# A Trainium2 decoder-layer kernel: expert weights made per four rows, and the gathers, routing and key queries of the expert stage interleaved more finely

## The chip, the cores and the metric

The kernel runs on one core of one Trainium2 chip. The metric is the device time of one execution, in microseconds. The engines are named as in the profile: PE is TensorE, DVE is VectorE, ACT is ScalarE, POOL is GpSimd, SP is SyncE. Each engine works through its own instructions in order, and semaphores are what order one engine against another.

## The reference

One decoder layer on 256 tokens of width 1024: RMS norm, a combined projection, two groups of attention heads, an output projection and the residual, then a second RMS norm and a feed-forward part that looks up experts. Only that last part, PEER, is touched by the change:

```python
q = (xc @ w_query).reshape(PEER_CHUNK, PEER_HEADS, 2, PEER_D_HALF)
sc = jnp.einsum('chpd,hpnd->chpn', q, sub_keys)
s1, i1 = lax.top_k(sc[:, :, 0], 16)
s2, i2 = lax.top_k(sc[:, :, 1], 16)
cand = s1[..., :, None] + s2[..., None, :]
best, pos = lax.top_k(cand.reshape(..., 256), 16)
experts = take_along_axis(i1 * 128 + i2, pos)
g = softmax(best)
h = gelu(einsum('cd,chkd->chk', xc, u[experts]))
out = einsum('chk,chkd->cd', h * g, v[experts])
```

There are 8 heads, and each token takes 16 experts per head out of 16,384. An expert has one row of 1024 floats in u and one in v. So each of the 256 tokens reads 128 rows of u and 128 rows of v: 256 x 256 x 4 KB = 268 MB in all, the bulk of what the kernel moves.

## The kernel before

Tokens lie on the 128 partitions, in two halves h. Attention and both projections come first and are not touched. In the expert stage a **gather** is one indirect DMA from GpSimd: for a head i, a half h and a rank s it fetches one row of u (or of v) for each of 128 tokens, 128 x 4 KB = 512 KB. There are 8 x 2 x 16 = 256 U gathers and 256 V gathers, numbered n from 0 in the order head, half, rank. Head i's rows are 32 i to 32 i + 31. The work on them:

- TensorE makes the key queries (L1157, 16 projections of a head's half-query, `hp` = 0 to 15, two a head) and their products with the sub keys (`key_scores`, L1143), one after another for all heads. ScalarE copies both out of PSUM (`query_evac`, `scores_evac`). Only then do the V products start on TensorE, which takes its instructions in order. A projection chunk in `w_raw` serves two `hp`; SyncE loads the next one when `w_used` says that a slot is free.
- VectorE does `route(i)` for a head: top 16 of the keys of both halves (`top_keys`, twice), the top 16 of the sums (`top_candidates`), and the expert numbers (`experts`). `expert_ready` lets GpSimd gather the head's rows.
- GpSimd issues U gather n (L361) once `u_used` frees its slot in a ring of `U_RING` = 8 rows, and V gather n (L370) once `v_used` frees its slot in a ring of `V_RING` = 6 rows. Work goes in units of 16 rows (one head and half). In the loop over units it alternates one U gather of unit u with one V gather of unit u - 1, so that V runs 16 rows behind U. A wait of either kind holds all gathers behind it.
- VectorE takes the dot product of each U row with the normed token (`dots`, L904, a multiply with a sum, its two inputs both in SBUF), 16 in a row, then `weights(u)`: it waits for ScalarE's gelu of the 16 dots and multiplies by the softmax gate. After each even unit it does `route` of the next head in one piece.
- ScalarE turns each weight into a diagonal matrix (`diag`, L601, ring of 8), and TensorE adds diag times V row into four PSUM banks (L1175): two products of 128x512 per row, each recorded as two matmuls, so four records a row. The product's end raises `v_used`.

At the end the PSUM banks are copied to SBUF and stored.

Of the kernel before, what the change touches and what calls it, by code (L numbers as in the profile page):

```python
# [34 lines left out]
COLS = 512  # L35
TOPK = 16
PEER_HEADS = 8
N_KEYS = 128
HP = PEER_HEADS * 2
# [4 lines left out]
W_LOADS = 4  # L44
# [9 lines left out]
QK_TENSOR = [2, 3, 0, 1]  # L54
INSTANCES = MOBA_HEADS + 2 * DIFF_HEADS
MIXES = MOBA_HEADS + DIFF_HEADS
U_RING = 8
V_RING = 6
DIAG_RING = 8
PAIRS = HALVES * TOPK  # L60
GATHERS = PEER_HEADS * PAIRS
UNITS = PEER_HEADS * HALVES
G1, G2, GQK, GSUB = 0, 8, 16, 20
N_GAINS = 21

# [1 line left out]
def layer(nc, x, norm1_g, w_in, moba_g, diff_g, diff_lambda, subln_g, w_out, norm2_g, w_query, sub_keys,  # L67
# [59 lines left out]
    sk_nat = over.put("sk_nat", [P, HP, P])  # L127
    logits = over.put("logits", [P, 2, 3 * P])
    probsT = over.put("probsT", [P, 2, 3 * P])
    lam_in = over.put("lam_in", [P, 4 * HEAD])  # L130
    lam_prod = over.put("lam_prod", [P, 2, HEAD])
    tiny = {}
# [10 lines left out]
    expd = over.put("expd", [P, 4, 3 * P])  # L143
    mixed = over.put("mixed", [P, 2, 3 * P])
    w_lo = over.put("w_lo", [P, W_PARTS, 4, COLS], F32R)
    assert over.at <= arena_at

    over = Region(routing_at)
# [21 lines left out]
    with keep:  # L170
        ps = [keep.enter_context(nc.psum_tensor(f"bank{i}", [P, COLS], F32)) for i in range(8)]

        def sem(name):
            return keep.enter_context(nc.semaphore(name))
# [75 lines left out]
        diag_ready = sem("diag_ready")  # L250
        v_used = sem("v_used")
        y_ready = [sem(f"y_ready{h}") for h in range(HALVES)]

        def need(eng, s, value):

# [66 lines left out]
        def _(pool):  # L322
# [33 lines left out]
            def gather_u(n):  # L356

                i, pair = divmod(n, PAIRS)
                h, s = divmod(pair, TOPK)
                need(pool, u_used, n - U_RING + 1)  # L360
                pool.indirect_dma_start(u_rows[:, n % U_RING, :], None, peer_u[0],  # L361
                                        bass.IndirectOffsetOnAxis(ap=expert[:, i, h, s:s + 1], axis=0))\
                    .then_inc(u_landed[n % U_RING], 16)

            def gather_v(n):

                i, pair = divmod(n, PAIRS)
                h, s = divmod(pair, TOPK)
                need(pool, v_used, n - V_RING + 1)
                pool.indirect_dma_start(v_rows[:, n % V_RING, :], None, peer_v[0],  # L370
                                        bass.IndirectOffsetOnAxis(ap=expert[:, i, h, s:s + 1], axis=0))\
                    .then_inc(v_landed[n % V_RING], 16)

            for u in range(UNITS + 1):
                if u < UNITS and u % HALVES == 0:
                    pool.wait_ge(expert_ready, u // HALVES + 1)
                for s in range(TOPK):
                    if u < UNITS:
                        gather_u(u * TOPK + s)
                    if u:  # L380
                        gather_v((u - 1) * TOPK + s)

        @block.scalar
        def _(act):
# [181 lines left out]
            def scores_evac(hp):  # L566
                act.wait_ge(scores_done, hp + 1)
                act.activation(scores[:, :, hp, :], ps[hp % 2][:, 0:SEQ].rearrange("p (h n) -> p h n", h=2), ACT.Copy)\  # L568
                   .then_inc(scores_ready, 1)
# [7 lines left out]
            for hp in range(HP):  # L577
                query_evac(hp)
                if hp == 0:
                    scores_evac(0)  # L580
                elif hp > 1:
                    scores_evac(hp - 1)
            scores_evac(HP - 1)
# [6 lines left out]
            def gelu(u):  # L590

                i, h = divmod(u, HALVES)
                act.wait_ge(u_used, (u + 1) * TOPK)
                act.activation(h_gelu[:, i, h, :], h_dot[:, i, h, :], ACT.Gelu).then_inc(gelu_done, 1)  # L594

            def diagonal(n):

                i, pair = divmod(n, PAIRS)
                h, s = divmod(pair, TOPK)
                need(act, v_used, n - DIAG_RING + 1)  # L600
                act.activation(diag[:, n % DIAG_RING, :], ident[:, :], ACT.Copy, scale=act_w[:, i, h, s:s + 1])\  # L601
                   .then_inc(diag_ready, 1)

            gate_exp(0)
            for u in range(UNITS):
                gelu(u)
                act.wait_ge(act_ready, u + 1)
                for n in range(u * TOPK, (u + 1) * TOPK):
                    diagonal(n)
                if u % HALVES == 0 and u // HALVES + 1 < PEER_HEADS:  # L610
                    gate_exp(u // HALVES + 1)

            act.wait_ge(v_used, GATHERS - TOPK)
            for c in range(2):
# [5 lines left out]
        def _(dve):  # L620
# [267 lines left out]
            def route(i):  # L888

                top_keys(2 * i)  # L890
                values_at, last = top_keys(2 * i + 1)
                last = top_candidates(i, values_at)
                dve.wait_ge(dve_step, last)
                experts(i)
                dve.tensor_tensor(gexp[:, :, i, :], best[:, :, i, :], best[:, :, i, 0:1].to_broadcast([P, HALVES, TOPK]),
                                  ALU.subtract).then_inc(gexp_in, 1)

            def dots(u):

                i, h = divmod(u, HALVES)  # L900
                for s in range(TOPK):
                    n = u * TOPK + s
# [6 lines left out]
            def weights(u):  # L909

                i, h = divmod(u, HALVES)
                if h == 0:
# [5 lines left out]
                dve.wait_ge(gelu_done, u + 1)  # L918
                dve.tensor_tensor(act_w[:, i, h, :], h_gelu[:, i, h, :], gate[:, i % 2, h, :], ALU.mult).then_inc(act_ready, 1)

            dve.wait_ge(iota_ready, 1)
            route(0)
            dve.wait_ge(xg_ready, HALVES)
            for u in range(UNITS):
                dots(u)
                weights(u)
                if u % HALVES == 0 and u // HALVES + 1 < PEER_HEADS:
                    route(u // HALVES + 1)

            dve.wait_ge(v_used, GATHERS)  # L930
            dve.tensor_copy(y_rows[:, 1, 0:COLS], ps[6][:, :]).then_inc(y_ready[1], 1)
# [2 lines left out]
        def _(pe):  # L934
# [209 lines left out]
                             start=True, stop=True)  # L1144
                ins.then_inc(scores_done, 1)

            for hp in range(HP):
                c = hp % 2
                j = PROJ_CHUNKS + 4 + hp // 2
                if c == 0:  # L1150
                    pe.wait_ge(w_loaded[j % W_LOADS], 16 * (j // W_LOADS + 1))
                if hp >= 2:
                    pe.wait_ge(query_ready, hp - 1)
                for k in range(KD):
# [4 lines left out]
                ins.then_inc(query_done, 1)  # L1159
                if c == 1:  # L1160
                    pe.wait_ge(query_done, hp + 1)
                    pe.sem_inc(w_used, 1)
                if hp == 0:
                    key_scores(0)
                elif hp > 1:
                    key_scores(hp - 1)
            key_scores(HP - 1)

            for u in range(UNITS):
                h = u % HALVES  # L1170
                for n in range(u * TOPK, (u + 1) * TOPK):
                    pe.wait_ge(diag_ready, n + 1)
                    pe.wait_ge(v_landed[n % V_RING], 16 * (n // V_RING + 1))
                    for c in range(2):
                        ins = mm(ps[4 + 2 * h + c][:, :], diag[:, n % DIAG_RING, :],  # L1175
                                 v_rows[:, n % V_RING, c * COLS:(c + 1) * COLS],
                                 start=False, stop=True, skip_group_check=True)
                    ins.then_inc(v_used, 1)

# [22 lines left out]
```

## Time and profile before

| what | value |
|---|---|
| median of 3 runs | 911.74 us |
| lowest, highest | 909.52, 918.73 us |
| span of the profiled execution | 900.1 us, 6762 instructions |
| busy in the span | PE 701.9, DVE 499.7, ACT 222.0, POOL 564.0 us |
| software DMA queue (the gathers) | 268.47 MB |

The runs are whole executions. The profiled execution is one more, and of it the span is known, from its first to its last instruction; its device time is not listed beside it. The median lies 11.64 us above the span, which is taken as what lies around it. Busy time of an engine says what it did, not what the kernel waited for.

### The profile page before, as it was taken

Reading aid. Unit: us, or ns where it says so; the run is one execution under the profiler, and the core shown is the slowest. Engines: PE = TensorE matmul, PEld = TensorE weight load, DVE = VectorE, ACT = ScalarE, POOL = GpSimd, SP = SyncE. Lnnn points to the kernel's source line nnn. Section 1 sums busy time; section 2 is a strip of 40 time slices with the busy share of each in tenths; the row PEclk is TensorE's granted clock in tenths of the full one; section 3 lists DMA queues with packets and bytes.
Section 4 is the critical chain, followed back from the end, with each engine's and each line's share of the span. In section 5 each row is a group of like instructions: output and inputs, shape, how many; then the busy total and the mean of one; then the engine's idle time right before and its main releaser. Section 6 shows DMA issues by size and latency. Waiting matters only on the chain.

```text
span 900.1 us, 6762 instructions
## 1 busy us (share of the span) xinstructions
PE 701.9 (78%) x2005; PEld 338.8 (38%) x2005; DVE 499.7 (56%) x1224; ACT 222.0 (25%) x504; POOL 564.0 (63%) x535
## 2 busy tenths in 40 slices
PE   5999998997777667776767677777676777777788
PEld 4877787884222222222222222222222222222233
DVE  5577724654644754485449444944493559444420
ACT  6568742123110111021202120212021202111111
POOL 6001000573777777777777777777787777777762
PEclk9999999998799999999999999999999999999999
DMA  8744221795799999999999999999999999999996
GB/s 324 265 163 152 88 67 48 252 399 226 226 389 381 386 355 410 409 409 350 381 380 384 340 409 410 384 361 374 382 357 361 409 410 379 388 409 410 409 378 222
DMA packets 91974, 297.88 MB, mean 331 GB/s; under 512 B 8721, under 2 KB 17058, under 8 KB 91938
## 3 DMA queue, kind: packets, MB, share of 16 engines
q0 software_dynamic: 73728, 268.47, 77.7%
q1 hardware_dynamic: 18210, 28.98, 9.5%
q8 instruction: 17, 0.28, 0.1%
q14 instruction: 19, 0.16, 0.0%
HBM read 296.36 MB, written 1.05 MB: 330 GB/s over the span
## 4 chain that ended last, share of the span: by engine, by line
POOL 33%; PE 27%; DMA 20%; issue 12%; DVE 5%; ACT 2%; SPq 0%; DVEq 0%
DMA v_rows<-in_peer_v_dram,expert 19%; POOL u_rows L361 17%; POOL v_rows L370 16%; PE bank L1175 10%; PE bank L1157 6%; PE bank L957 5%; PE bank L1015 1%; PE bank L1143 1%; DVE w_lo L644 1%; DMA u_rows<-in_peer_u_dram,expert 1%; DVE t_nmax L674 1%; DVE logits L671 1%; DMA x_sb<-in_x_dram 0%; PE bank L942 0%; ACT diag L601 0%
## 5 line engine op out<-in xcount | busy, mean ns | idle before, releaser
L1175 PE MATMUL bank<-v_rows,diag 128*128 128x512 f32 x1024 | 506.9, 623 | 178.7 <-DMA v_rows<-in_peer_v_dram,expert 163.4
L904 DVE CUSTOM_DVE_ANT_0 u_rows<-u_rows,xg 128x1024 f32<-128x1024 f32 x256 | 310.4, 1226 | 283.7 <-DMA u_rows<-in_peer_u_dram,expert 283.4
L1175 PEld LDWEIGHTS bank<-v_rows,diag 128*128 128x128 f32 x1024 | 179.6, 193 | 505.4 <-issue 328.5
L361 POOL DMA_INDIRECT u_rows<-in_peer_u_dram,expert x256 | 269.3, 1052 | 105.1 <-issue 77.5
L370 POOL DMA_INDIRECT v_rows<-in_peer_v_dram,expert x256 | 274.7, 1073 | 94.9 <-issue 53.9
L601 ACT ACTIVATE diag<-ident,act_w 128x128 f32<-128x128 f32 x256 | 90.5, 394 | 273.3 <-PE bank L1175 267.4
L594 ACT ACTIVATE h_gelu<-h_dot 128x16 f32<-128x16 f32 x16 | 3.4, 216 | 282.0 <-DVE h_dot L904 282.0
L1157 PE MATMUL bank<-featT,w_raw 128*128 128x256 f32 x256 | 58.0, 380 | 0.7 <-ACT featT L563 0.4
L1157 PEld LDWEIGHTS bank<-featT,w_raw 128*128 128x128 f32 x256 | 47.4, 190 | 7.0 <-issue 1.3
L279 POOL TENSOR_TENSOR normed<-qk_raw,t_qk_rs 128x512 f32<-128x512 f32 x4 | 4.1, 1043 | 67.8 <-DVE t_qk_rs L740 67.8
L957 PE MATMUL bank<-w_hi,xn_hi 128*128 128x512 f32 x112 | 45.5, 406 | 0.2 <-DVE xn_lo L767 0.2
L957 PE MATMUL bank<-w_hi,xn_lo 128*128 128x512 f32 x112 | 43.8, 391 | 0.0
L957 PE MATMUL bank<-w_lo,xn_hi 128*128 128x512 f32 x112 | 43.7, 390 | 0.0
L644 DVE TENSOR_TENSOR w_lo<-w_raw,w_hi 128x2048 fp32r<-128x2048 f32 x16 | 36.6, 2289 | 9.8 <-ACT w_hi L396 9.8
L353 POOL IOTA iota<- 128x512 bf16 x1 | 0.6, 631 | 54.0 <-PE bank L1132 54.0
L396 ACT ACTIVATE w_hi<-w_raw 128x2048 fp32r<-128x2048 f32 x16 | 30.5, 1919 | 7.9 <-PE bank L957 4.1
L957 PEld LDWEIGHTS bank<-w_hi,xn_hi 128*128 128x128 f32 x112 | 21.0, 188 | 6.9 <-issue 3.1
L957 PEld LDWEIGHTS bank<-w_hi,xn_lo 128*128 128x128 f32 x112 | 21.0, 188 | 4.5
L957 PEld LDWEIGHTS bank<-w_lo,xn_hi 128*128 128x128 f32 x112 | 21.1, 188 | 4.1 <-issue 0.2
L904 DVE DVE_READ_ACCUMULATOR2_ANT h_dot<- 128x1 f32 x256 | 20.8, 81 | 0.0
L828 DVE MAX8 key_val<-scores 128x8 f32<-128x128 f32 x64 | 15.2, 280 | 7.6 <-ACT scores L568 7.6
L575 ACT ACTIVATE qT<-bank 128x256 f32<-128x256 f32 x16 | 6.1, 383 | 49.8 <-PE bank L1157 49.8
(149 smaller groups left out, 407.1 us busy)
## 6 DMA issues: line engine op xcount, KB each, us to landing
w_raw<-in_w_in_dram SPq DMA_DIRECT2D x12, 1024.0 KB, 8.4
w_raw<-in_peer_w_query_dram SPq DMA_DIRECT2D x8, 1024.0 KB, 5.4
w_raw<-in_w_out_dram SPq DMA_DIRECT2D x4, 1024.0 KB, 5.2
u_rows<-in_peer_u_dram,expert POOLq DMA_INDIRECT x256, 6.6
v_rows<-in_peer_v_dram,expert POOLq DMA_INDIRECT x256, 6.6
x_sb<-in_x_dram SPq DMA_DIRECT2D x2, 512.0 KB, 3.7
out_dram<-y_rows SPq DMA_DIRECT2D x2, 512.0 KB, 4.6
g_row<-in_norm_g_dram SPq DMA_DIRECT2D x1, 512.0 KB, 13.4
```

Of the source, the lines that this page charges most:

```text
L361: pool.indirect_dma_start(u_rows[:, n % U_RING, :], None, peer_u[0], bass.IndirectOffsetOnAxis(ap=expert[:, i, h, s:s + 1], axis=0))\
L370: pool.indirect_dma_start(v_rows[:, n % V_RING, :], None, peer_v[0], bass.IndirectOffsetOnAxis(ap=expert[:, i, h, s:s + 1], axis=0))\
L396: act.activation(w_hi[:, j % W_PARTS, :, :].rearrange("p k n -> p (k n)"), w_raw[:, j % W_LOADS, :], ACT.Copy)\
L601: act.activation(diag[:, n % DIAG_RING, :], ident[:, :], ACT.Copy, scale=act_w[:, i, h, s:s + 1])\
L644: dve.tensor_tensor(w_lo[:, j % W_PARTS, :, :].rearrange("p k n -> p (k n)"), w_raw[:, j % W_LOADS, :], w_hi[:, j % W_PARTS, :, :].rearran ...
L671: link(dve.tensor_tensor(logits[:, row, :], ps[bank][:, 0:3 * P], bias_t[:, table, :], ALU.add))
L674: ins = dve.tensor_reduce(tiny["nmax"][:, c:c + 1], logits[:, row, lo:hi], AX.X, ALU.max, negate=True)
L828: at[h] = mark(dve.max(val[h], scores[:, h, hp, :]))
L904: dve.tensor_tensor_reduce(out=u_rows[:, n % U_RING, :], in0=u_rows[:, n % U_RING, :], in1=xg[:, h, :], scale=1.0, scalar=0.0, op0=ALU.mul ...
L957: ins = mm(ps[bank][:, :], a[:, 4 * kh + k, h * P:(h + 1) * P], b[:, j % W_PARTS, k, :], start=start and k == 0 and n == 0, stop=stop and ...
L1157: ins = mm(ps[2 + hp % 2][:, 0:SEQ], w_raw[:, j % W_LOADS, 2 * k * P + c * P:2 * k * P + (c + 1) * P], featT[:, k, :], start=k == 0, stop= ...
L1175: ins = mm(ps[4 + 2 * h + c][:, :], diag[:, n % DIAG_RING, :], v_rows[:, n % V_RING, c * COLS:(c + 1) * COLS], start=False, stop=True, ski ...
```

## The change

- `U_RING` goes from 8 to 10 rows, `V_RING` from 6 to 8. To make room, three tiles of the attention part (`sk_nat`, `logits`, `probsT`) lie in the region that the rings use later.
- GpSimd alternates U gather n with V gather n - 8 (`LAG`) instead of n - 16.
- Weights are made in groups of four rows (`GROUP`): gelu on 4 dots, 64 times instead of 16. VectorE multiplies a group's weights after the dots of the next group.
- `route` is cut into four parts (the two `top_keys`, `top_candidates`, `experts` with the softmax input), placed after the dots of groups 1 to 4 of the eight groups of the head before.
- TensorE projects only `hp` 0 to 3 (heads 0 and 1) ahead of the V products. The projections and key scores of heads 2 to 7 stand between the V products of the head that is two earlier: half a projection after rows 1, 3, 5 and 7, key scores after rows 8 and 12. ScalarE's copies for them stand between its diagonals. The next chunk's load is released after row 12. Within heads 0 and 1 both projections now come ahead of both key scores.

```diff
-U_RING = 8
-V_RING = 6
+U_RING = 10
+V_RING = 8
+GROUP = 4
+LAG = 8
...
-            for u in range(UNITS + 1):
-                if u < UNITS and u % HALVES == 0:
-                    pool.wait_ge(expert_ready, u // HALVES + 1)
-                for s in range(TOPK):
-                    if u < UNITS:
-                        gather_u(u * TOPK + s)
-                    if u:
-                        gather_v((u - 1) * TOPK + s)
+            for n in range(GATHERS + LAG):
+                if n < GATHERS:
+                    if n % PAIRS == 0:
+                        pool.wait_ge(expert_ready, n // PAIRS + 1)
+                    gather_u(n)
+                if n >= LAG:
+                    gather_v(n - LAG)
...
+            for g in range(GROUPS + 1):
+                if g < GROUPS:
+                    gelu(g)
+                if g:
+                    act.wait_ge(act_ready, g)
+                    for n in range((g - 1) * GROUP, g * GROUP):
+                        diagonal(n)
+                        i, at = divmod(n, PAIRS)
+                        if i + 2 < PEER_HEADS:
+                            if at in (QUERY_EVAC, QUERY_EVAC + 4):
+                                query_evac(2 * (i + 2) + (at - QUERY_EVAC) // 4)
+                            if at in (SCORES_EVAC, SCORES_EVAC + 4):
+                                scores_evac(2 * (i + 2) + (at - SCORES_EVAC) // 4)
+                i, at = divmod(g, HEAD_GROUPS)
+                if at == 6 and i + 1 < PEER_HEADS:
+                    gate_exp(i + 1)
...
-            for u in range(UNITS):
-                dots(u)
-                weights(u)
-                if u % HALVES == 0 and u // HALVES + 1 < PEER_HEADS:
-                    route(u // HALVES + 1)
+            for g in range(GROUPS):
+                dots(g)
+                if g:
+                    weights(g - 1)
+                i, at = divmod(g, HEAD_GROUPS)
+                if 1 <= at <= 4 and i + 1 < PEER_HEADS:
+                    route(i + 1, at - 1)
+            weights(GROUPS - 1)
...
+            query(0, range(KD))
+            query(1, range(KD))
+            key_scores(0)
+            key_scores(1)
+            w_done(1)
+            query(2, range(KD))
+            query(3, range(KD))
+            key_scores(2)
+            key_scores(3)
+            w_done(3)
...
+                ins.then_inc(v_used, 1)
 
+                hp, at = 2 * (i + 2), n % PAIRS
+                if hp < HP:
+                    if at in (1, 5):
+                        query(hp + at // 4, range(4))
+                    if at in (3, 7):
+                        query(hp + at // 4, range(4, KD))
+                    if at in (8, 12):
+                        key_scores(hp + (at - 8) // 4)
+                    if at == 12:
+                        w_done(hp + 1)
```

## Rows read from the trace of the kernel before

**Rows 1.** The page's 40 slices of 22.5 us: GpSimd busy tenths, DMA rate.

```profile
POOL 6001000573777777777777777777787777777762
...
GB/s 324 265 163 152 88 67 48 252 399 226 226 389 381 386 355 410 409 409 350 381 380 384 340 409 410 384 361 374 382 357 361 409 410 379 388 409 410 409 378 222
```

**Rows 2.** The page's costliest groups: V products and dots.

```profile
L1175 PE MATMUL bank<-v_rows,diag 128*128 128x512 f32 x1024 | 506.9, 623 | 178.7 <-DMA v_rows<-in_peer_v_dram,expert 163.4
L904 DVE CUSTOM_DVE_ANT_0 u_rows<-u_rows,xg 128x1024 f32<-128x1024 f32 x256 | 310.4, 1226 | 283.7 <-DMA u_rows<-in_peer_u_dram,expert 283.4
```

**Rows 3.** Timeline of GpSimd (start us, us): first gathers, the stop.

```profile
165.76 1.16 POOL L361 DMA_INDIRECT u_rows<-in_peer_u_dram,expert  x1 [22.51 <-DVE expert L885]
...
178.08 1.19 POOL L361 DMA_INDIRECT u_rows<-in_peer_u_dram,expert  x1 [0.30 <-issue]
...
218.94 0.94 POOL L370 DMA_INDIRECT v_rows<-in_peer_v_dram,expert  x1 [10.98 <-PE bank L1175]
...
227.53 1.68 POOL L361 DMA_INDIRECT u_rows<-in_peer_u_dram,expert  x1 [5.09 <-DVE h_dot L904]
229.52 1.99 POOL L370 DMA_INDIRECT v_rows<-in_peer_v_dram,expert  x1 [0.30 <-issue]
```

**Rows 4.** Windows: busy us (count) by engine, granted clock, DMA share, GB/s.

```profile
350.00:370.00 20.00, 14.58 (x31) 4.82 (x29) 9.86 (x16) 3.21 (x8) 15.42 (x16) 1.00 1.03 409
433.00:468.00 35.00, 24.48 (x51) 8.32 (x49) 16.03 (x26) 5.06 (x15) 27.35 (x26) 1.00 1.00 377
488.00:498.00 10.00, 7.53 (x16) 2.41 (x14) 9.53 (x18) 1.61 (x4) 8.51 (x5) 1.00 0.89 316
```

**Rows 5.** Timeline, VectorE dots beside gathers: steady stretch, then one collision.

```profile
352.68 1.22 DVE L904 CUSTOM_DVE_ANT_0 u_rows<-u_rows,xg 128x1024 f32<-128x1024 f32 x1 [1.33 <-DMA u_rows<-in_peer_u_dram,expert]
...
353.70 1.01 POOL L361 DMA_INDIRECT u_rows<-in_peer_u_dram,expert  x1 [0.30 <-issue]
...
441.57 1.23 DVE L904 CUSTOM_DVE_ANT_0 u_rows<-u_rows,xg 128x1024 f32<-128x1024 f32 x1 [2.02 <-DMA u_rows<-in_peer_u_dram,expert]
...
441.90 1.70 POOL L370 DMA_INDIRECT v_rows<-in_peer_v_dram,expert  x1 [0.30 <-PE bank L1175]
```

**Rows 6.** Timeline, dots one behind another after routing, beside gathers.

```profile
402.84 1.22 DVE L904 CUSTOM_DVE_ANT_0 u_rows<-u_rows,xg 128x1024 f32<-128x1024 f32 x1
402.88 1.99 POOL L361 DMA_INDIRECT u_rows<-in_peer_u_dram,expert  x1 [0.30 <-issue]
...
403.98 1.22 DVE L904 CUSTOM_DVE_ANT_0 u_rows<-u_rows,xg 128x1024 f32<-128x1024 f32 x1
```

**Rows 7.** Windows of the U gathers alone, then of the V gathers alone.

```profile
229.52:858.80 629.28, 238.38 (x230) 0.98 1.00 383
...
229.52:858.80 629.28, 250.32 (x231) 0.98 1.00 383
```

**Rows 8.** Timeline, head 0's routing: second projection, its keys, candidates, experts.

```profile
147.62 3.62 PE L1157 MATMUL bank<-featT,w_raw 128*128 128x256 f32 x16
...
156.14 0.49 DVE L828 MAX8 key_val<-scores 128x8 f32<-128x128 f32 x2 [5.39 <-ACT scores L568]
...
158.49 0.17 DVE L840 TENSOR_TENSOR cand<-key_val 128x32 f32<-128x32 f32 x1
...
161.57 0.20 DVE L862 CAST key_idb<-key_idx 128x64 bf16<-128x64 uint32 x1
```

**Rows 9.** Timeline, the end: last U gather, last products, copy to SBUF.

```profile
858.82 1.01 POOL L361 DMA_INDIRECT u_rows<-in_peer_u_dram,expert  x1 [0.30 <-issue]
...
866.87 29.42 PE L1175 MATMUL bank<-v_rows,diag 128*128 128x512 f32 x68 [0.61 <-DMA v_rows<-in_peer_v_dram,expert]
...
896.33 0.60 ACT L617 ACTIVATE y_rows<-bank 128x512 f32<-128x512 f32 x1 [12.36 <-PE bank L1175]
```

**Rows 10.** Timeline of TensorE: a V product after an idle stretch.

```profile
234.88 3.75 PE L1175 MATMUL bank<-v_rows,diag 128*128 128x512 f32 x4 [3.35 <-DMA v_rows<-in_peer_v_dram,expert]
```

**Rows 11.** The view of one line, V gathers: time to landing.

```profile
DMA to landing us min/median/max: 4.3/6.6/8.1
```

More of the change, by code:

```diff
@@ L56 @@
 MIXES = MOBA_HEADS + DIFF_HEADS
-U_RING = 8
-V_RING = 6
+U_RING = 10
+V_RING = 8
 DIAG_RING = 8
+GROUP = 4
+LAG = 8
+QUERY_EVAC = 7
+SCORES_EVAC = 12
 PAIRS = HALVES * TOPK
 GATHERS = PEER_HEADS * PAIRS
-UNITS = PEER_HEADS * HALVES
+GROUPS = GATHERS // GROUP
+HEAD_GROUPS = PAIRS // GROUP
 G1, G2, GQK, GSUB = 0, 8, 16, 20
@@ L145, in layer @@
     w_lo = over.put("w_lo", [P, W_PARTS, 4, COLS], F32R)
+    sk_nat = over.put("sk_nat", [P, HP, P])
+    logits = over.put("logits", [P, 2, 3 * P])
+    probsT = over.put("probsT", [P, 2, 3 * P])
     assert over.at <= arena_at
@@ L252, in layer, with place @@
         y_ready = [sem(f"y_ready{h}") for h in range(HALVES)]
+        def place(n):
+            i, pair = divmod(n, PAIRS)
+            return i, *divmod(pair, TOPK)
         def need(eng, s, value):
@@ L575, in query_evac @@
                 act.activation(qT[:, hp % 2, :], ps[2 + hp % 2][:, 0:SEQ], ACT.Copy).then_inc(query_ready, 1)
-            for hp in range(HP):
+            for hp in range(4):
                 query_evac(hp)
-                if hp == 0:
+                if hp == 1:
                     scores_evac(0)
-                elif hp > 1:
-                    scores_evac(hp - 1)
-            scores_evac(HP - 1)
+                    scores_evac(1)
+            scores_evac(2)
+            scores_evac(3)
             def gate_exp(i):
@@ L588, in gate_exp, with gelu @@
                 act.activation(gexp[:, :, i, :], gexp[:, :, i, :], ACT.Exp).then_inc(gexp_done, 1)
[L590 to L594, printed above, removed]
+            def gelu(g):
+                i, h, s = place(g * GROUP)
+                act.wait_ge(u_used, (g + 1) * GROUP)
+                act.activation(h_gelu[:, i, h, s:s + GROUP], h_dot[:, i, h, s:s + GROUP], ACT.Gelu).then_inc(gelu_done, 1)
             def diagonal(n):
-                i, pair = divmod(n, PAIRS)
-                h, s = divmod(pair, TOPK)
+                i, h, s = place(n)
                 need(act, v_used, n - DIAG_RING + 1)
@@ L604, in _ @@
             gate_exp(0)
-            for u in range(UNITS):
[L606 to L609, printed above, removed]
-                if u % HALVES == 0 and u // HALVES + 1 < PEER_HEADS:
-                    gate_exp(u // HALVES + 1)
+            for g in range(GROUPS + 1):
[14 more added lines that the diff above has]
+                    gate_exp(i + 1)
             act.wait_ge(v_used, GATHERS - TOPK)
@@ L886, in experts, with route, dots @@
                                          ALU.mult, ALU.add).then_inc(expert_ready, 1)
[L888 to L902, printed above, removed]
+            values_at, positions_at = [0] * HP, [0] * PEER_HEADS
+            def route(i, part):
+                if part < 2:
+                    values_at[2 * i + part] = top_keys(2 * i + part)[0]
+                elif part == 2:
+                    positions_at[i] = top_candidates(i, values_at[2 * i + 1])
+                else:
+                    dve.wait_ge(dve_step, positions_at[i])
+                    experts(i)
+                    dve.tensor_tensor(gexp[:, :, i, :], best[:, :, i, :], best[:, :, i, 0:1].to_broadcast([P, HALVES, TOPK]),
+                                      ALU.subtract).then_inc(gexp_in, 1)
+            def dots(g):
+                for n in range(g * GROUP, (g + 1) * GROUP):
+                    i, h, s = place(n)
                     dve.wait_ge(u_landed[n % U_RING], 16 * (n // U_RING + 1))
@@ L907, in dots, with weights @@
                        .then_inc(u_used, 1)
-            def weights(u):
-                i, h = divmod(u, HALVES)
-                if h == 0:
+            def weights(g):
+                i, h, s = place(g * GROUP)
+                if g % HEAD_GROUPS == 0:
                     dve.wait_ge(gexp_done, i + 1)
@@ L917, in weights @@
                                            gsum[:, 1, i, :].unsqueeze(2).to_broadcast([P, HALVES, TOPK]), ALU.mult))
-                dve.wait_ge(gelu_done, u + 1)
-                dve.tensor_tensor(act_w[:, i, h, :], h_gelu[:, i, h, :], gate[:, i % 2, h, :], ALU.mult).then_inc(act_ready, 1)
+                dve.wait_ge(gelu_done, g + 1)
+                dve.tensor_tensor(act_w[:, i, h, s:s + GROUP], h_gelu[:, i, h, s:s + GROUP],
+                                  gate[:, i % 2, h, s:s + GROUP], ALU.mult).then_inc(act_ready, 1)
             dve.wait_ge(iota_ready, 1)
-            route(0)
+            for part in range(4):
+                route(0, part)
             dve.wait_ge(xg_ready, HALVES)
-            for u in range(UNITS):
-                dots(u)
-                weights(u)
-                if u % HALVES == 0 and u // HALVES + 1 < PEER_HEADS:
-                    route(u // HALVES + 1)
+            for g in range(GROUPS):
[6 more added lines that the diff above has]
+            weights(GROUPS - 1)
             dve.wait_ge(v_used, GATHERS)
@@ L1145, in key_scores, with query @@
                 ins.then_inc(scores_done, 1)
-            for hp in range(HP):
+            def query(hp, ks):
                 c = hp % 2
                 j = PROJ_CHUNKS + 4 + hp // 2
[L1150 to L1154, printed above, removed]
+                if ks[0] == 0:
+                    if c == 0:
+                        pe.wait_ge(w_loaded[j % W_LOADS], 16 * (j // W_LOADS + 1))
+                    if hp >= 2:
+                        pe.wait_ge(query_ready, hp - 1)
+                for k in ks:
                     if hp == 0 and k % 2 == 0:
@@ L1158, in _ @@
                              featT[:, k, :], start=k == 0, stop=k == KD - 1)
[L1159 to L1178, printed above, removed]
+                if ks[-1] == KD - 1:
+                    ins.then_inc(query_done, 1)
@@ new lines, in w_done @@
+            def w_done(hp):
+                pe.wait_ge(query_done, hp + 1)
+                pe.sem_inc(w_used, 1)
+            query(0, range(KD))
[8 more added lines that the diff above has]
+            w_done(3)
+            for n in range(GATHERS):
+                i, h, s = place(n)
+                pe.wait_ge(diag_ready, n + 1)
+                pe.wait_ge(v_landed[n % V_RING], 16 * (n // V_RING + 1))
+                for c in range(2):
+                    ins = mm(ps[4 + 2 * h + c][:, :], diag[:, n % DIAG_RING, :],
+                             v_rows[:, n % V_RING, c * COLS:(c + 1) * COLS],
+                             start=False, stop=True, skip_group_check=True)
+                ins.then_inc(v_used, 1)
[9 more added lines that the diff above has]
+                        w_done(hp + 1)
```

3 lines of the change are left out of this document (removed).

## The prediction

> **What bounds the kernel now.** I read the page's slices first [rows 1]. GpSimd's gathers start in the eighth slice (157 us); from the twelfth on it is busy seven or eight tenths and the DMA moves 340 to 410 GB/s. Between them, in slice 10, GpSimd falls to 3 tenths, and the rate to 226 GB/s for two slices. So four fifths of the span are the gathers. The groups [rows 2] say that the two engines that use the rows mostly wait for them: the dots' idle time, 283 us, ends with a U row's landing, and 163 of TensorE's 179 us with a V row's. The next question is whether GpSimd or the DMA sets the pace.
>
> The windows answer it [rows 4]. At 350 to 370 us the DMA moves 409 GB/s at a share of 1.03, so it is full: a row of 512 KB takes 1.28 us and a pair (one U, one V) 2.56. GpSimd's own floor is a hair under that: 0.94 us a gather and 0.30 to the next, 2.48 a pair [rows 3]. But the mean over 229.52 to 858.82 is 461 gathers in 629.3 us, 1.365 each: 1.06 us busy and 0.30 between [rows 7]. GpSimd never stops there; its gathers are longer than 0.94.
>
> The timeline says why. In the full stretch a U gather meets the last of a dot and takes 1.01. A gather that starts while a dot runs ends 0.80 us behind the dot: dot from 441.57 to 442.80, gather from 441.90 to 443.60 [rows 5]. With dots back to back each gather waits for one to end and the cycle is 1.99 + 0.30 = 2.29 [rows 6]. The Trainium skill (SBUF — State Buffer, "SBUF: two separate sides") has the shared port as an exclusive lock, the later one fully blocked. The trace agrees as to the gathers; if the dots too waited for whole gathers, a pair would be 1.22 + 2 x 0.94 + 0.60 = 3.7 us and not 2.56, so the lock holds only part of a gather.
>
> Two stretches are apart from this pace: the **stop** at 208 to 227, where GpSimd idles 10.98 us for the first V product (TensorE is still at queries) and then 5.09 us for the dots (VectorE is in `route`) [rows 3]; and the **end**, 858.82 to 896.3, where only V gathers are left and TensorE's 1.73 us a row (29.42 us for 17 rows) sets the rate [rows 9].
>
> **The change part by part**, along GpSimd's queue.
>
> Start. The second projection runs 147.62 to 151.24, yet its keys are read at 156.14, because its scores stand behind projection 2 [rows 8]. Now scores 0 and 1 follow projection 1. Without the gap ahead of it that ends at about 150.1; evacuations and scores bring the first `top_keys` to 151.5; one takes 158.49 - 156.14 = 2.35 us, the second starts at about 154.0, 2.1 us earlier. The first gather, 165.76 [rows 3], moves to **163.6**.
>
> U alone. 16 U gathers alone become 8. The first eight took 178.08 - 165.76 = **12.3 us** [rows 3], beside loads of query weights, of which two of four now come later.
>
> Stop. V gather 8 would be the first to wait for V product 0. It is due 16 gathers after 175.9, at 197 us. Product 0 wants dots 0 to 7, a group's weights and a diagonal: by about 185. TensorE is then free since about 161, so the wait and the stop go (16 us). TensorE starts cold: a product after idle took 3.75 us instead of 1.95 [rows 10]. With 12 us in hand and a ring of 8 a few such rows cost nothing.
>
> Pairs. From U gather 8 to U gather 255 there are 247 pairs, 494 gathers. At today's 1.365 they take 674 us. What moves that pace:
> - `route` in parts. It takes 2 x 2.35 + 3.08 (158.49 to 161.57) + about 4 = 11.8 us [rows 8], and holds the dots: eight back to back follow, four gathers of 1.05 us excess, 4.2 us a head. In parts nothing of it goes: 11.8 us of dots' delay still make about 7 displaced dots. At 0.52 us each (1.05 per two dots, rows 6) that is 3.6 us. Single delays of 1 us can hide in the DMA queue, whose landing time of 6.6 us lies 2.3 above its least [rows 11]. I take 1 us a head off, 7 us.
> - The pace between them has two modes in the trace, full DMA at 1.28 a gather and 377 GB/s, 1.39 a gather [rows 4], where dots hit every third V gather. Which one follows a disturbance I can't read; bounds 1.29 and 1.40.
> - 48 more gelus (ACT has idle time; it makes diagonals up to 8 ahead) and 48 more weight products of 0.18 us. These fall into the 1.33 us for which VectorE waits before each dot [rows 5]. Uncovered: 8 us of VectorE, nothing of GpSimd. As two-input operations they can hold a gather 0.18 us; bounds 0 and 8 us, taken 0, since few meet one.
> - Projections between products: a head costs TensorE 32 x 1.73 + 2 x 3.6 + 1.2 = 64 us of the 82 to 88 that its gathers take, at worst 2 to 3 us late against 11 us of slack in V's ring (8 x 2.7 less landing and product). ScalarE's diagonal behind a `query_evac` waits for TensorE's third row; eight diagonals are ahead. 0 us; without the cover the bound is still 64 a head, below the gathers.
> - Rings of 10 and 8: GpSimd shows no wait for a slot outside the stop, so 0. What they give is cover.
> - Two query chunks of 1 MB now load beside full gathers: 0 if there is slack, 5.1 us at 409 GB/s; taken 2.5.
>
> So the pairs take 494 x 1.35 = **667 us**, and the last U gather starts at 163.6 + 12.3 + 667 + 2.5 = 845.4.
>
> End. It leaves 9 V gathers at 1.28. The first lands at about +7.9 us; nine products of 1.73 follow: TensorE ends at +23.5. Copy and store take 900.1 - 896.3 = 3.8 [rows 9]. That is **27.3** where 41.3 stands now.
>
> Sum: 845.4 + 27.3 = 872.7 us of span; with 11.64 around it, **884 us**, against 911.74. The same by part: start -2.1; the first 33 gathers, 63.8 us up to 229.52 with the stop in them [rows 3], now 12.3 + 25 x 1.35 = 46.1, so -17.7; eight V gathers more ahead of the last U gather, +10.8; pace of the other 461, -7; loads +2.5; end -14. That is -27.4.
>
> **The rivals.**
> 1. **Full DMA takes over.** With short disturbances the mode of 1.28 holds. For it: 350 to 370, and VectorE no longer stays away 12 us. Against: half the dots of a head are displaced. At 1.295: 494 x 0.055 = 27 less, 857 us. Chance 0.20.
> 2. **More collisions.** Each part kicks the phase between dots and gathers, and 377 GB/s becomes the rule: 1.40, 25 more, 909 us. Chance 0.18.
> 3. **Slower: dots back to back become normal.** If 20 of 32 dots of a head cost 0.52 us (pair 3.0) and 12 stay at 2.73, the pair is 2.90: 1.45 x 494 puts 49 us on the sum, 933 us. Beyond 1.425 a gather it passes 921. Against: after 4 us of routing VectorE needs only two or three dots to catch up. Chance 0.07.
> 4. **The stop stays**, from a late first weight or cold TensorE: 16 us back, 900. Chance 0.05.
>
> The skill's table on the same page ("A bandwidth-pool intuition that's wrong") gives a core about 358 GB/s from HBM. By it 268 MB need 750 us and no finer order would help; the time would stay at or above today's. The row with 409 GB/s over 20 us stands against it, so this rival gets no chance of its own.
>
> **How the numbers follow.** The forecast 884 has 0.50. The range runs from 858, the full-DMA case, to 909, the colliding one; it leaves out the rest of rival 3 and part of the two edges. A change under 1% (9 us) is about what can't be told from none here. Faster by over 1% (below 902.6): 0.50 + 0.20 + 0.05 + 0.06 of rival 2 = 0.81. Within: 0.12 of rival 2 and 0.01 = 0.13. Slower: 0.06.
>
> **What would show it.** The first gather at about 163.6; GpSimd with no idle over 1 us after it; V gathers from about 176; gathers 1.29 to 1.40 us apart on the mean, 1.35 as forecast; four short runs of two or three back-to-back dots a head in place of one of eight, gathers of 1.99 fewer; last U gather near 845 with under 28 us behind it. Wrong would be: GpSimd waiting for a ring or for `expert_ready`, VectorE waiting for gelu behind a ScalarE that is held by a query, or a mean gather above 1.12 us busy.

## The result, and the profile after

| | before | changed |
|---|---|---|
| median | 911.46 us (4 runs) | 888.88 us (4 runs, 887.01 to 890.03) |
| ratio of the changed kernel to the one before | | 0.973, 95% interval 0.9674 to 0.9785 |
| span of the profiled execution | 900.1 us | 888.2 us |

The changed kernel is 22.6 us faster, 2.7%. The forecast was 884 with a range of 858 to 909. (Medians are over all executions; the ratios here and below leave out every execution that took over 1.5% longer than the fastest of its kernel.) The profiled execution of it took 890.03 us, 1.8 around its span. For the one before, its executions beside the later runs have spans too, and on the first two chips each lies 1.7 to 2.0 us under its time (906.41 with 904.5, for one). So its profiled execution, with a span of 900.1, was some 9 us shorter than its median, and the 11.64 us that the prediction put around the span were mostly that difference.

Where the time went is read best along GpSimd's queue. First the page's slices, as in [rows 1]:

```profile
POOL 6001000577777777777777777777777777777772
...
GB/s 329 268 149 150 88 71 65 237 365 367 404 410 371 356 404 409 377 346 365 376 368 370 400 388 372 352 409 408 389 369 372 373 377 369 382 372 370 402 409 255
```

The hole in the tenth and eleventh slices is gone. The level of the rest is not higher: it moves between 350 and 410 as before. The timeline of GpSimd gives the start, which answers to [rows 3]:

```profile
162.97 1.16 POOL L371 DMA_INDIRECT u_rows<-in_peer_u_dram,expert  x1 [19.73 <-DVE expert L902]
...
174.20 0.99 POOL L371 DMA_INDIRECT u_rows<-in_peer_u_dram,expert  x1 [0.30 <-issue]
175.50 1.39 POOL L380 DMA_INDIRECT v_rows<-in_peer_v_dram,expert  x1 [0.30 <-issue]
```

174.20 is U gather 8, behind the eight that go alone; 175.50 is V gather 0. From there to the end no gather has more than 0.31 us of idle ahead of it. The windows of the U gathers alone and of the V gathers alone, from the first V gather to the last U gather, answer to [rows 7]:

```profile
175.50:860.61 685.11, 251.31 (x247) 0.99 1.00 381
...
175.50:860.61 685.11, 283.48 (x247) 0.99 1.00 381
```

These windows hold 494 gathers, of which the last one only starts at their end. So from V gather 0 to U gather 255 there are 493 intervals in 685.11 us, and from U gather 8, where the prediction begins its pairs, 494 in 686.41: 1.39 us each, 1.085 of it busy. The profiled execution of the kernel before had 1.365. The end, as in [rows 9]:

```profile
860.61 1.02 POOL L371 DMA_INDIRECT u_rows<-in_peer_u_dram,expert  x1 [0.30 <-issue]
...
868.66 15.69 PE L1210 MATMUL bank<-v_rows,diag 128*128 128x512 f32 x36 [0.61 <-DMA v_rows<-in_peer_v_dram,expert]
...
884.38 0.60 ACT L634 ACTIVATE y_rows<-bank 128x512 f32<-128x512 f32 x1 [12.35 <-PE bank L1210]
```

Nine products (36 records) end the work, where there were 17. 27.6 us lie behind the last U gather, where there were 41.3.

The sum of the changed kernel, term by term, forecast against measured:

| stretch | forecast | measured |
|---|---|---|
| to the first gather | 163.6 | 162.97 |
| eight U gathers alone | 12.3 | 11.23 |
| 494 gathers in pairs | 667 | 686.41 |
| query loads beside them | 2.5 | in the line above |
| behind the last U gather | 27.3 | 27.6 |
| span | 872.7 | 888.2 |
| around the span | 11.64 | 1.8 |

Two errors, 15.5 us too little in the span and 9.8 too much around it, stand against each other in the 884.

The timeline of TensorE shows the cold start that rival 4 feared:

```profile
182.05 5.76 PE L1210 MATMUL bank<-v_rows,diag 128*128 128x512 f32 x8 [22.73 <-DMA v_rows<-in_peer_v_dram,expert]
187.65 1.89 PE L1184 MATMUL bank<-featT,w_raw 128*128 128x256 f32 x8
189.38 3.60 PE L1210 MATMUL bank<-v_rows,diag 128*128 128x512 f32 x8
```

After 22.73 us of idle the first two rows take 5.76 us, at a mean granted clock of 0.64 from 182 to 188 us, and the next two 3.60, at 1.00 from 188 us on; half a projection between them costs 1.7 us. V gather 8 found its slot free: it went out at 199.10, 0.30 us behind the gather ahead of it.

And the timeline of dots and gathers shows what holds the pace, after a part of the routing:

```profile
371.34 1.20 DVE L924 CUSTOM_DVE_ANT_0 u_rows<-u_rows,xg 128x1024 f32<-128x1024 f32 x1
371.35 2.00 POOL L380 DMA_INDIRECT v_rows<-in_peer_v_dram,expert  x1 [0.31 <-PE bank L1210]
```

The gather that starts with the dot takes 2.00 us instead of 0.94. The runs of seven to nine dots back to back are gone (there were seven of them), but V gathers are busy 1.148 us on the mean of this stretch (283.48 / 247), against 1.084 before (250.32 / 231 in [rows 7]), while U gathers go from 1.036 to 1.022 (251.31 / 246, without the one at the end). Fewer gathers are held for a whole dot (15 take over 1.9 us instead of 25), but more are held for a part of one: 86 take over 1.3 us instead of 62.

### The profile page after: what moved, and what is told of

It is laid out like the page before. It is cut to its first block, busy times and chain, and to the rows that moved or that the text cites. A ratio compares the mean times of both kernels' runs of the same rounds, so it can differ in the third digit from the quotient of the medians.

```text
span 888.2 us, 6905 instructions
## 1 busy us (share of the span) xinstructions
PE 687.9 (77%) x2005; PEld 340.3 (38%) x2005; DVE 504.3 (57%) x1272; ACT 215.6 (24%) x552; POOL 574.4 (65%) x535
## 4 chain that ended last, share of the span: by engine, by line
DMA 29%; POOL 29%; PE 24%; issue 11%; DVE 5%; ACT 1%; SPq 0%; POOLq 0%; DVEq 0%
DMA v_rows<-in_peer_v_dram,expert 29%; POOL u_rows L371 15%; POOL v_rows L380 14%; PE bank L1210 13%; PE bank L982 5%; PE bank L1184 2%; PE bank L1040 1%; DVE w_lo L661 1%; DVE t_nmax L691 1%; DVE logits L688 1%; DMA x_sb<-in_x_dram 0%; PE bank L967 0%; PE bank L1005 0%; DVE expd L716 0%; PE bank L1001 0%
## 5 line engine op out<-in xcount | busy, mean ns | idle before, releaser
L1210 PE MATMUL bank<-v_rows,diag 128*128 128x512 f32 x1024 | 499.0, 613 | 183.5 <-DMA v_rows<-in_peer_v_dram,expert 176.3
L380 POOL DMA_INDIRECT v_rows<-in_peer_v_dram,expert x256 | 292.1, 1141 | 78.1 <-issue 46.3
L371 POOL DMA_INDIRECT u_rows<-in_peer_u_dram,expert x256 | 262.1, 1024 | 97.5 <-issue 77.8
L603 ACT ACTIVATE h_gelu<-h_dot 128x4 f32<-128x4 f32 x64 | 13.1, 205 | 551.9 <-DVE h_dot L924 551.9
L609 ACT ACTIVATE diag<-ident,act_w 128x128 f32<-128x128 f32 x256 | 81.9, 387 | 4.1 <-DVE act_w L939 4.1
L848 DVE FIND_INDEX8 key_idx<-key_val,scores 128x8 uint32<-128x128 f32 x64 | 17.7, 283 | 0.0
```

The costliest lines, as they stand in the source:

```text
L603: act.activation(h_gelu[:, i, h, s:s + GROUP], h_dot[:, i, h, s:s + GROUP], ACT.Gelu).then_inc(gelu_done, 1)
L848: last = mark(dve.max_index(key_idx[:, h, hp, 8 * r:8 * r + 8], val[h], scores[:, h, hp, :]))
```

## The experiments

The theory was: the stop and the end gave the gain; the pace between is set by dots that hold gathers, and the change left that alone. Rivals were that the projections between products or the cut routing slow the pairs, and that the pace is the DMA's own. The first four kernels each undo one part of the changed kernel; they share one chip and its runs of the kernel before (median 911.2 us).

**All queries ahead of the V products again.**

```diff
-            query(0, range(KD))
-            query(1, range(KD))
-            key_scores(0)
-            key_scores(1)
-            w_done(1)
...
+            for i in range(PEER_HEADS):
+                query(2 * i, range(KD))
+                query(2 * i + 1, range(KD))
+                key_scores(2 * i)
+                key_scores(2 * i + 1)
+                w_done(2 * i + 1)
```

> Undoes the placing of the queries alone: TensorE makes all 16 projections ahead of the first V product. Theory (the stop is TensorE's queue, the pace between is set by dots that hold gathers): the stop comes back at V gather 8, near 197 us, until the first product near 208 us, so 10 to 16 us of idle GpSimd and a time 8 to 14 us above the changed kernel's 889, about 900. The pace of the pairs stays at 1.37 to 1.40 us a gather. Rival (projections between V products are what slows the pairs to 1.39): the pace falls to 1.35 or less and the time comes out at or below 889.

Measured: 904.67 us median, 0.9931 of the kernel before (0.9887 to 0.9976). Its timeline of GpSimd:

```profile
195.41 0.94 POOL L371 DMA_INDIRECT u_rows<-in_peer_u_dram,expert  x1 [0.30 <-issue]
215.04 1.03 POOL L380 DMA_INDIRECT v_rows<-in_peer_v_dram,expert  x1 [18.69 <-PE bank L1204]
```

The stop is back, in one piece of 18.69 us at V gather 8, and the time is 15.8 us above the changed kernel's; both are just above the expected 10 to 16 and 8 to 14. TensorE's first V product came at 211.12, after 4.23 us of waiting for its diagonal, and it was cold (granted clock 0.57 from 211 to 215 us): V gather 8 went out at 215.04, after it. Without the stop the 493 intervals of the pairs are 1.388 us each, as in the changed kernel (1.390). So the projections cost the pairs nothing that shows, and moving them is worth the stop.

**The routing in one piece again**, after the dots of group 3.

```diff
-                if 1 <= at <= 4 and i + 1 < PEER_HEADS:
-                    route(i + 1, at - 1)
+                if at == 3 and i + 1 < PEER_HEADS:
+                    for part in range(4):
+                        route(i + 1, part)
```

> Undoes the cutting of the routing alone: all four parts stand after the dots of group 3. Theory (a dot that is displaced costs the same, in one run or in four): pace 1.37 to 1.41 us a gather as in the changed kernel, time within 1% of 889. Rival (the four kicks of a head knock the dots out of the mode of 1.28 a gather): the pace falls to 1.365 or lower, 12 us or more off, 877 or less.

Measured: 880.23 us (878.24 to 885.16), 0.9675 (0.9622 to 0.9727), at a pace of 1.362. Here the theory missed: the time lies at the edge of the 1%, and the pace is better by 0.028 and below the 1.37 expected. It is the pace that the rival named, but not its time. The interval of the ratio overlaps that of the changed kernel (0.9674 to 0.9785). The page's groups of gathers:

```profile
L371 POOL DMA_INDIRECT u_rows<-in_peer_u_dram,expert x256 | 266.2, 1040 | 97.5 <-issue 77.7
L380 POOL DMA_INDIRECT v_rows<-in_peer_v_dram,expert x256 | 275.7, 1077 | 78.1 <-issue 48.2
```

V gathers take 1.077 us instead of the changed kernel's 1.141 over the whole execution, U gathers 1.040 instead of 1.024. 58 gathers take over 1.3 us, where the changed kernel has 86.

**V 16 rows behind U again.**

```diff
-LAG = 8
+LAG = 16
```

> Undoes the lag alone: V gathers 16 behind U gathers again. Theory (end and start are worth 14 and 18 us less 11 for the V gathers that move): 17 V gathers are left after the last U gather and go at TensorE's 1.73 us a row, so the part behind the last U gather grows from 27.6 to about 41, and the last U gather starts about 11 us less 2 to 3 for slower single U gathers earlier: 893 to 896 us, up 4 to 7. Rival (the lag is worth nothing, since the work is the same): within 2 us of 889.

Measured: 892.47 us, 0.9839 (0.9743 to 0.9934), within 1 us of the expectation; one of its four executions took 905.57. The last U gather starts at 848.97, 11.6 us before the changed kernel's, and 41.2 us follow it; 17 products stand in a row at the end of TensorE's timeline:

```profile
856.99 29.42 PE L1210 MATMUL bank<-v_rows,diag 128*128 128x512 f32 x68 [0.60 <-DMA v_rows<-in_peer_v_dram,expert]
```

The pace is 1.386. So the lag moves 14 us out of the end and puts 11 into the pairs, as the traces show. The net of 3.6 us between the medians is smaller than the noise: the intervals of the two ratios overlap.

**Rings of 8 and 6 rows again**, in the same memory.

```diff
-U_RING = 10
-V_RING = 8
+U_RING = 8
+V_RING = 6
```

> Undoes the ring sizes alone: 8 and 6 rows are used. Theory (GpSimd never waits for a slot): no idle of GpSimd over 1 us behind the first gather, time within 1% of 889. Rival (the larger rings are what covers the projections between products and the routing): idle on GpSimd before V or U gathers, over 9 us in sum, 898 or more.

Measured: 892.78 us (888.96 to 900.38), 0.9801 (0.972 to 0.9882), pace 1.394. Only the last three V gathers wait, 1.6 us at most, which is over the 1 us expected but lies in the end and not in the pairs. The rings are worth nothing here that can be told from chance.

The next three test what sets the pace; they share another chip (kernel before 911.9 us there).

**Half dots.**

```diff
-... tensor_tensor_reduce(out=u_rows[:, n % U_RING, :], in0=u_rows[:, n % U_RING, :], in1=xg[:, h, :],
+... tensor_tensor_reduce(out=u_rows[:, n % U_RING, 0:COLS], in0=u_rows[:, n % U_RING, 0:COLS], in1=xg[:, h, 0:COLS],
```

> Leaves out half of each dot product: the dots take columns 0 to 511 of a row only, all gathers and products stay. A dot is then some 0.65 us instead of 1.22. Theory (a gather is held until the dot that runs at its start is over): fewer and shorter delays, GpSimd's gathers 0.94 to 0.98 us busy on the mean, pace at the full DMA's 1.28 to 1.31 us a gather, time 840 to 850. Rival (the pace of 1.39 is the DMA's or GpSimd's own, and VectorE has nothing to do with it): pace 1.37 to 1.40, time within 1% of 889.

Measured: 847.21 us, 0.9309 (0.9243 to 0.9375), pace 1.283, with gathers of 0.968 and 0.963 us on the mean: all as the theory said. The dots take 0.69 us. This kernel leaves out half of every dot, so it doesn't compute the reference.

**The same dots with one operand in PSUM.**

```diff
-... in0=u_rows[:, n % U_RING, :], in1=xg[:, h, :],
+... in0=u_rows[:, n % U_RING, :].rearrange("p (a b) -> p a b", a=2),
+    in1=ps[3][:, :].unsqueeze(1).to_broadcast([P, 2, COLS]),
```

> Changes the dots: each multiplies a full U row of 1024 columns by 512 columns that lie in a PSUM bank, taken twice, instead of the tokens' 1024 columns in SBUF; the queries use one bank instead of two. The dots keep their length or grow a little, but have one SBUF input. Theory (what holds a gather is the dot's second SBUF input): no gather is held any more, all close to 0.94 us, pace 1.28 to 1.30, time 835 to 850, although VectorE is as busy. Rival (any long VectorE instruction on SBUF holds a gather, by its length): pace stays at 1.36 to 1.40, time 880 or more.

Measured: 848.75 us, 0.9318 (0.9227 to 0.941), pace 1.283. One of its four executions took 3826.44 us and has no explanation; the others lie between 847.34 and 848.76. The bank holds no tokens, so this kernel doesn't compute the reference either. With one bank for the queries, ScalarE's copies of them also move up, from behind the diagonals of rows 7 and 11 to those of rows 4 and 8. Its timeline, where a gather starts with a dot as it did above:

```profile
501.26 1.22 DVE L924 CUSTOM_DVE_ANT_1 u_rows<-u_rows,bank 128x1024 f32<-128x1024 f32 x1 [1.32 <-DMA u_rows<-in_peer_u_dram,expert]
501.27 0.94 POOL L371 DMA_INDIRECT u_rows<-in_peer_u_dram,expert  x1 [0.30 <-issue]
```

The dot is as long as before, 1.22 us, and the gather is not held. The page's groups say it of all of them:

```profile
L380 POOL DMA_INDIRECT v_rows<-in_peer_v_dram,expert x256 | 241.1, 942 | 105.2 <-PE bank L1209 64.1
L371 POOL DMA_INDIRECT u_rows<-in_peer_u_dram,expert x256 | 242.2, 946 | 98.5 <-issue 72.6
```

So what holds a gather is the dot's second SBUF input, not its length as such, and that is worth about 40 us here. (The dot is recorded as another instruction here, ANT_1 for ANT_0. The kernel that keeps the tokens in PSUM, further down, has ANT_0 with the bank as input, and its gathers are not held either.) The holds themselves were more than 40 us: the changed kernel's 512 gathers are busy 73 us more than 0.94 us each would be. Without them the pairs are 53 us shorter, down to the DMA's pace, but 39.0 us lie behind the last U gather instead of 27.6, since the DMA is further behind. The Trainium skill (SBUF — State Buffer, "Who interferes with whom") says that a DVE instruction with two SBUF inputs contends with a GpSimd instruction that reads SBUF; the gather reads its expert numbers there, and these two runs agree. GpSimd is then ahead of the DMA: the view of the V gathers' line gives the time to landing as

```profile
DMA to landing us min/median/max: 7.1/17.6/19.1
```

against 5.4/6.4/9.1 in the changed kernel. Ten gathers wait over 0.5 us for their slot, 1.4 us at most, and the floor is the DMA: 512 KB in 1.283 us is 409 GB/s.

**The routing in two parts**, after groups 2 and 4.

```diff
-                if 1 <= at <= 4 and i + 1 < PEER_HEADS:
-                    route(i + 1, at - 1)
+                if at in (2, 4) and i + 1 < PEER_HEADS:
+                    for part in (at - 2, at - 1):
+                        route(i + 1, part)
```

> Cuts the routing in two parts instead of four (after the dots of groups 2 and 4). Theory since the run with the whole routing (each stay of VectorE away from the dots moves their phase against the gathers, so the pace gets worse with the number of parts): between 880 and 889, about 884, pace 1.37 to 1.385. Rival (where the whole routing stands, not the number of parts, made that run faster; or chance): no order by the number of parts, 888 or more, or 878 or less.

Measured: 894.26 us, 0.9826 (0.973 to 0.9922), pace 1.391. That is what the rival said: there is no order by the number of parts, with 880 for one, 894 for two, 889 for four.

The last five runs, three and then two, fell on two further chips. The kernel before took 979.31 us on the first of them (959.28 to 1006.21) and 983.09 us on the second (966.46 to 1001.0), 7 and 8% above the first two chips by the medians. A kernel that keeps the tokens in PSUM and computes all of the reference was made for them:

```diff
+            def xg_load(unit):
+                for c in range(2):
+                    act.activation(ps[c][:, :], xg[:, unit % HALVES, c * COLS:(c + 1) * COLS], ACT.Copy).then_inc(xg_in, 1)
...
                 if g < GROUPS:
                     gelu(g)
+                    if g % 4 == 3 and g + 1 < GROUPS:
+                        xg_load(g // 4 + 1)
...
             def dots(g):
+                if g % 4 == 0:
+                    dve.wait_ge(xg_in, 2 * (g // 4 + 1))
...
-                                             ... in1=xg[:, h, :],
+                                             ... in1=low[:, :],
```

`low` is banks 0 and 1 as one tile; from `hp` = 2 on, queries use bank 2 and key scores bank 3, and TensorE waits for the copy of the one before. ScalarE's query copies stand behind rows 4 and 8, as in the run with one operand in PSUM.

> The changed kernel once more, beside the two below on the same chip: what one and the same program differs by from one chip and one profiled execution to another. Theory (the pace of 1.36 to 1.40 is a matter of how dots and gathers happen to meet, and differs by some us from execution to execution): median 885 to 893. Rival (each program has its pace): within 1 us of 889, pace 1.39.

Measured: 920.25 us, 0.9546 (0.9491 to 0.96).

> The kernel with the routing in one piece once more. If cutting the routing costs 9 us, as its first run said: 880 again, and 8 to 10 us under the changed kernel on the same chip. If that was a chance of one chip: within 4 us of the changed kernel.

Measured: 936.08 us, 0.9686 (0.9618 to 0.9755): here it is slower than the changed kernel, with intervals that lie apart, where its first run was faster. Its profiled execution took 945.97 us, 10 us over the median, so its trace is not used.

> The whole computation, with the normed tokens of the present half (xg) copied by ScalarE into two PSUM banks every 16 rows, so that the dots read one operand from SBUF and one from PSUM; queries and key scores use one bank each behind the first head. Theory (the dots' second SBUF input is what holds the gathers): pace 1.283, 846 to 853 us, 0.93 to 0.935 of the kernel before, the copies and the waits for them (16 times some 1.4 us of VectorE) cost GpSimd nothing. Rival (the stop of the dots at each half, or the projections behind one bank, hold the gathers instead): idle of GpSimd of 10 us or more in sum and 860 or more.

Measured: 919.16 us, 0.9517 (0.9458 to 0.9576).

> The kernel with the normed tokens in PSUM once more, since on the chip of its first run every kernel, the one before the change too, was 3 to 7% slower than elsewhere and GpSimd stopped 1 to 5 us at a time for V's ring. On a chip where the kernel before takes 903 to 920 us: 846 to 853 us, pace 1.283, by the theory that the dots' second SBUF input is what holds the gathers. If the copies by half or the projections behind one bank cost: 860 or more.

Measured: 916.36 us, 0.9387 (0.932 to 0.9453), beside

> The changed kernel beside it, on the same chip: 885 to 893 us where the kernel before takes 903 to 920, with gathers at 1.37 to 1.40 us apart.

Measured: 920.54 us, 0.9442 (0.9388 to 0.9497).

None of these five came out at its expected time. The waits in the changed kernel's trace on the first of the two chips, between 200 and 840 us (who waited for whom: us in total, times, longest), show that the chip slows this kernel too:

```profile
ACT qT L584 <- remote: 72.1, 8, 19.9
...
POOL v_rows L380 <- PE bank L1210: 27.5, 46, 4.7
POOL v_rows L380 <- remote: 20.0, 12, 3.8
...
DVE best L868 <- remote: 12.2, 5, 3.2
```

"remote" is a releaser that the trace doesn't name. In the same view of the changed kernel's first trace, in the section on the result, no releaser is "remote", ScalarE waits 3.4 us at most for a query (`qT`), and GpSimd never over 0.3 us. Why these chips differ is not known. In the PSUM kernel's trace beside it the gathers are not held, which is its purpose (the page's groups):

```profile
L390 POOL DMA_INDIRECT v_rows<-in_peer_v_dram,expert x256 | 240.4, 939 | 185.1 <-PE bank L1233 71.3
L381 POOL DMA_INDIRECT u_rows<-in_peer_u_dram,expert x256 | 240.5, 940 | 97.8 <-issue 75.5
```

but GpSimd stops for V's ring, for 5.27 us here and 5.32 us at most:

```profile
463.72 0.94 POOL L390 DMA_INDIRECT v_rows<-in_peer_v_dram,expert  x1 [5.27 <-PE bank L1233]
```

On these chips the PSUM kernel is 1 us and 4 us faster than the changed one, less than either interval. In the pairs, GpSimd's waits of over 0.5 us add up to 103 and 96 us in its two traces, against 33 and 35 us in the changed kernel's beside them. The dots waited up to 8.8 us for the copy of the tokens, five times and 35 us in sum on the first chip. That is the idle which the rival of its expectation named, so these runs don't separate what the chip costs from what the copies and the single bank cost. That the kernel would reach 850 us where the kernel before takes 911 is argued from the run with one PSUM operand; it was not measured.

## Why the prediction was right, point by point

**The bound.** GpSimd sets the pace and dots hold its gathers: right, and shown by two runs. Without the hold the pace is 1.283 us, the full DMA's 1.28 of the prediction.

**Start.** First gather 2.8 us earlier, forecast 2.1. **U alone** 11.23, forecast 12.3. **Stop**: gone, and put back by the run that puts the queries first. **End**: 27.6, forecast 27.3; the run with the old lag has 41.2 again, today's 41.3 of the prediction.

**Pairs.** This term was mis-sized: 494 x 1.35 = 667 against 686.4, 1.39 each. 7 us of the 19 missing are the step "I take 1 us a head off, 7 us": cutting the routing took nothing off that shows. The other 12 are the pace it was taken from, 1.365, read from one execution that was faster than its kernel's median (see below). The long runs of held gathers went, and shorter holds on V gathers came in their place: the mean V gather went from 1.084 to 1.148 us busy. (Four runs of two or three dots a head were forecast; the trace has 17 in all.) The prediction's own count, 7 displaced dots instead of 8 in each head, expects no gain either; the credit for delays hiding in the DMA queue has none to show. Rival 2 (each part of the routing disturbs the pairs, 1.40 a gather) comes nearest to what the pairs did, 1.39 with 86 held gathers instead of 62, but whether the parts are the cause is open.

**Around the span.** The 11.64 us were not what lies around it but mainly the distance of one execution from the median. With 1.8 around the forecast would have been 874.5, 14 us short and still in its range.

The two errors may have a common root. If the kernel before in its median execution has a span of 909.5, and if all of the difference lies in the pairs, its pace there would be 1.365 + 9.4/461 = 1.385, close to the changed kernel's 1.39. Then the change is worth: start -2.8; the first 33 gathers, 63.8 us, now 11.2 + 25 x 1.39 = 46.0, so -17.8; eight V gathers more in the pairs +11.1; the pace of the other 461, +2; end 41.3 to 27.6, -13.7. That is -21.2 in the span, against 22.6 between the medians (the profiled execution of the changed kernel was itself 1.2 over its median). By this the change left the pace alone. It is argued, not shown: there is no trace of a median execution of the kernel before. That the two errors nearly cancelled, so that the forecast lies 5 us from the result, is luck.

**Nothing for rings, gelus, weights, projections:** for the rings nothing else could be told (892.78 against 888.88, with overlapping intervals of the ratios), and for the projections it held (pace 1.388 without them between the products). Gelus and weights were not tried alone.

**Open.** Whether routing in one piece is better: 880 against 889, which were measured apart with overlapping intervals, 936 against 920 on one chip, and two parts at 894. These runs don't settle it. Open as well is what a kernel that computes all of the reference with its tokens in PSUM would take on a chip like the first two.

## What to carry to other kernels

Look first for the engine that never stops, and then at why its instructions are longer than their shortest: here GpSimd lost 73 us inside its gathers, not between them. An operand moved to PSUM took that away, in a test kernel that doesn't compute the reference, and brought 40 us; moving work around did not. Removing a stop and shortening a tail are gains that could be counted from the queue to within a few microseconds here; the credit for smoother interleaving could not. And take what lies around a span from an execution that has both numbers, not from a median beside another execution's span.

## What the runs showed of the hardware

A gather that starts while a two-input dot runs ends 0.80 us after the dot's end (371.35 to 373.35 beside a dot that ends at 372.54); with the second input in PSUM it takes 0.94 us beside a dot of the same 1.22 us. With gathers free, the DMA holds 409 GB/s nearly to the end, with 17.6 us from issue to landing; a ring of 8 rows at 2.57 us a pair (20.5 us, an estimate of how long a slot may stay taken) is then barely deep enough, and V gathers begin to wait. And two chips of the four in the experiments ran the kernel before at medians of 979 and 983 us instead of 911 and 912, and in the changed kernel's traces there ScalarE waits up to 20 us and GpSimd up to 4.5 us for releasers that the trace doesn't name; there the changed kernel's ratio gives a gain of 4.5 and 5.6% instead of 2.7.
